# A macaron encoder block on one core: feed-forward openings in eight plain products with norms by token halves, x in row tiles, and the closing projection by token halves

## The reference, cut to what matters

```python
x = x + 0.5 * swiglu(rmsnorm(x, ffn1_norm), ffn1_w_gate, ffn1_w_up, ffn1_w_down)
h = rmsnorm(x, mix_norm)                      # one projection of h feeds both branches
merged = sigmoid(gate_a) * window_attention(...) + sigmoid(gate_b) * rwkv7(...)
x = x + merged @ w_out                        # "project-out"
x = x + cross_attention(rmsnorm(x, cross_norm), rmsnorm(mem, mem_norm))   # ends with @ w_co
x = x + 0.5 * swiglu(rmsnorm(x, ffn2_norm), ffn2_w_gate, ffn2_w_up, ffn2_w_down)
return rmsnorm(x, final_norm)
# rmsnorm(x, g) = x * rsqrt(mean(x * x) + 1e-6) * g
# swiglu(h, wg, wu, wd) = (silu(h @ wg) * (h @ wu)) @ wd
```

## Time and profile before

| | us |
|---|---|
| three runs: median (lowest to highest) | 3220.22 (3218.71 to 3220.97) |
| the profiled execution: its time | 3219.02 |
| the profiled execution: its span, first to last instruction | 3217.2 |

### The profile page before, as it was taken

How to read it: one execution, slowest core, us unless ns; L and a number is a source line. 1 busy time by engine, 2 the same in 40 slices (tenths; PEclk the granted TensorE clock), 3 DMA queues, 4 the chain that set the end, 5 groups by cost and what they waited for, 6 DMA issues and landing times. The chain is left out here.

```text
span 3217.2 us, 61692 instructions
## 1 busy us (share of the span) xinstructions
PE 2943.0 (91%) x26984; PEld 2412.2 (75%) x26984; DVE 1621.0 (50%) x1767; ACT 1087.4 (34%) x1780; POOL 1353.7 (42%) x705
## 2 busy tenths in 40 slices
PE   3799999996899999999999998899995799999995
PEld 2688888885677878778787887686774688887885
DVE  5654443445146666555666665243224645543445
ACT  2433333223234434334443333342212333333221
POOL 1344444443255555444555454462131344444441
PEclk7999999998999999999999999899997899999997
DMA  3222224442421211131121212351002222234441
GB/s 143 69 94 96 83 105 147 144 147 49 175 62 51 59 58 58 37 108 47 46 61 53 63 43 74 116 160 46 26 27 79 69 79 85 98 109 145 143 147 69
DMA packets 260169, 279.12 MB, mean 87 GB/s; under 512 B 13504, under 2 KB 213312, under 8 KB 257728
## 3 DMA queue, kind: packets, MB, share of 16 engines
q1 hardware_dynamic: 259904, 275.20, 26.2%
HBM read 224.83 MB, written 50.33 MB: 86 GB/s over the span
## 5 line engine op out<-in xcount | busy, mean ns | idle before, releaser
L483 POOL TENSOR_TENSOR w_low<-ffn_work,w_high 128x1024 fp32r<-128x1024 f32 x182 | 444.9, 2445 | 668.7 <-ACT w_high L556 395.4
L523 PE MATMUL bank<-h_high,w_high 128*128 128x512 f32 x1232 | 484.8, 393 | 59.1 <-DVE h_low L667 34.9
L523 PE MATMUL bank<-h_low,w_high 128*128 128x512 f32 x1232 | 483.4, 392 | 0.0
L523 PE MATMUL bank<-h_high,w_low 128*128 128x512 f32 x1232 | 483.4, 392 | 0.0
L1228 POOL TENSOR_TENSOR mix_panel_low<-arena,mix_panel_high 128x1024 fp32r<-128x1024 f32 x114 | 276.3, 2425 | 406.2 <-ACT mix_panel_high L1605 406.2
L1334 PE MATMUL bank<-mix_h_high,mix_panel_high 128*128 128x512 f32 (+1 forms) x896 | 357.7, 399 | 21.1 <-POOL mix_panel_low L1228 16.0
L1334 PE MATMUL bank<-mix_h_low,mix_panel_high 128*128 128x512 f32 (+1 forms) x896 | 342.0, 382 | 0.0
L1334 PE MATMUL bank<-mix_h_high,mix_panel_low 128*128 128x512 f32 (+1 forms) x896 | 340.7, 380 | 0.0
L714 DVE TENSOR_TENSOR h_low<-ffn_work,h_high 128x512 fp32r<-128x512 f32 x88 | 204.4, 2323 | 250.4 <-ACT h_high L571 250.4
L523 PEld LDWEIGHTS bank<-h_high,w_high 128*128 128x128 f32 x1232 | 234.1, 190 | 112.2 <-issue 61.4
L540 PE MATMUL bank<-h_high,w_high 128*128 128x512 f32 x704 | 274.8, 390 | 4.4 <-DVE h_low L714 4.4
(11 more groups left out here) (276 smaller groups left out, 5784.4 us busy)
## 6 DMA issues: line engine op xcount, KB each, us to landing
arena<-w_in SPq DMA_DIRECT2D x96, 512.0 KB, 3.8
ffn_work<-w_down SPq DMA_DIRECT2D x88, 512.0 KB, 3.6
a_spill<-ffn_work SPq DMA_DIRECT2D x88, 256.0 KB, 2.2
ffn_work<-a_spill SPq DMA_DIRECT2D x88, 256.0 KB, 2.6
ffn_work<-w_gate SPq DMA_DIRECT2D x12, 1024.0 KB, 5.7
ffn_work<-w_up SPq DMA_DIRECT2D x12, 1024.0 KB, 8.2
arena<-w_gate SPq DMA_DIRECT2D x10, 1024.0 KB, 5.6
arena<-w_up SPq DMA_DIRECT2D x10, 1024.0 KB, 8.2
```

Of the source, the lines that this page charges most:

```text
L483: nc.gpsimd.tensor_tensor(slot(w[1], q), src, slot(w[0], q).bitcast(F32), ALU.subtract).then_inc(s_low, 1)
L523: last = mm(bank[:, bk, :], w[wp][:, q % RING, kt, e], h[hp][:, k, kt], start=fresh and kt + wp + hp == 0, stop=kt == KT // 2 - 1 and wp = ...
```

## The change

It does four things.

- The first pair of each feed-forward is made of eight plain products (`FIRST`) of five weight panels; pairs 2 to 11 stay as they are. The five panels are rounded in the order A11, A12, A21, A22 and A11 again. The T sums are made later, beside these products, T2 in place.
- The norm at a feed-forward's opening is done by token halves. In the second feed-forward the first half's norm, the load of the first weights and the first panel's two parts lie in the cross stage; the block of the feed-forward begins with the second half's sums (`nrm[1]`).
- x comes in eight tiles of 128 rows, three places in turn; ACT squares a row tile with an accumulated sum, so the first feed-forward's norm needs no squares of xT and no sums on PE. The block ahead of it is gone: its work stands in the feed-forward's block (`front`). The first weights come in two halves of the columns, the constants other than the identity later. x goes to `x_spill` in parts (`keep_x`).
- The closing projection keeps panels 0 and 1 for both halves and then goes through panels 2 to 7 for the first half of the tokens and again for the second: 14 units instead of 8 panels. In project-out and here DVE, not POOL, makes the panels' low parts.

`lowered(q)` is q + 1, less one in the second feed-forward. Beside this, buffers that were opened in the mixer and cross stages are opened once for the whole kernel, and the constant `keep` is made from 64 columns by one copy.

The diff, cut to this core:

```diff
...
+FIRST_PANELS = [A11, A12, A21, A22, A11]
+C11, C21, C22, C12 = (0, 1), (4, 5), (6, 7), (2, 3)
+FIRST = [(0, B11, C11, True), (1, B21, C11, False), (2, B11, C21, True), (3, B21, C21, False),
+         (1, B22, C12, True), (3, B22, C22, True), (2, B12, C22, False), (4, B12, C12, False)]
+NQ0 = len(FIRST_PANELS)
...
+            def load_rows():
+                def tile(t):
+                    if t >= 3:
+                        sp.wait_ge(s_sq, t - 2)
+                    sp.dma_start(tiles[t % 3], d["x"][t * P:(t + 1) * P, :]).then_inc(s_tile[t % 3], 16)
+
+                def first_weights(fh):
+                    for e, src in enumerate((wg, wu)):
+                        sp.dma_start(raw[0][:, :, e, fh * P:(fh + 1) * P],
+                                     src[:, :, fh * P:(fh + 1) * P]).then_inc(s_first[fh], 16)
+
+                def keep_x(j):
+                    sp.wait_ge(s_placed, 4 * j + 4)
+                    cols = slice(2 * j * P, 2 * (j + 1) * P)
+                    sp.dma_start(x_view[:, :, cols], xT[:, :, cols]).then_inc(s_kept_x[j // 2], 16)
+
+                at, n = where["ident"]
+                sp.dma_start(cst[:, at:at + n], d["consts"][:, at:at + n]).then_inc(s_ident, 16)
+                for t in range(3):
+                    tile(t)
+                sp.dma_start(par[:], d["params"].rearrange("p (a b) -> p a b", a=NPAR)).then_inc(s_par, 16)
+                first_weights(0)
+                tile(3)
+                keep_x(0)
+                tile(4)
+                keep_x(1)
+                for t in range(5, 8):
+                    tile(t)
+                first_weights(1)
+                sp.dma_start(cst[:, n:], d["consts"][:, n:]).then_inc(s_rest, 16)
+                sp.dma_start(par_u[:], d["params_u"][:, :]).then_inc(s_rest, 16)
+                keep_x(2)
+                keep_x(3)
+
+            if front:
+                load_rows()
+            keep_act(0, 0)
+            keep_act(0, 2)
+            sp.wait_ge(s_blow, low_at["T2"])
+            sp.wait_ge(s_bsum, sums_before["T2"])
             load_group(1)
-            for g in range(GROUPS):
-                keep_act(g, 0, 0, 0, post[0])
-                keep_act(g, 1, 1, 1, post[4])
+            sp.wait_ge(s_low, lowered(NQ0 - 1))
+            load_group(2)
+            keep_act(0, 1)
...
+            if front:
+                nc.gpsimd.memset(minus_half_c[:], -0.5).then_inc(s_eps, 1)
+                pool.wait_ge(s_eps, 1)
+                nrm[0].pool_root(pool)
+                subtract_low(0, block_of(0, FIRST_PANELS[0]))
+            else:
+                nrm[1].pool_root(pool)
+            for q in range(1, NQ0):
+                subtract_low(q, block_of(0, FIRST_PANELS[q]))
+                if front and q == 1:
+                    nrm[1].pool_root(pool)
...
+            def turn_tile(t):
+                pe.wait_ge(s_tile[t % 3], 16 * (t // 3 + 1))
+                for j in range(2):
+                    if t < 4:
+                        b = (2 * t + j) % 6
+                        if t >= 3:
+                            pe.wait_ge(s_placed, 2 * (t - 3) + j + 1)
+                    else:
+                        b = 2 + j
+                        pe.wait_ge(s_placed, 2 * (t - 1) + j + 1)
+                    for i in range(4):
+                        kt = 4 * j + i
+                        last = nc.tensor.transpose(bank[:, b, i * P:(i + 1) * P],
+                                                   tiles[t % 3][:, kt * P:(kt + 1) * P], c("ident"))
+                    last.then_inc(s_turned, 1)
+
+            def first_product(r):
+                q, k, banks, fresh = FIRST[r]
+                closing = r in (1, 3, 6, 7)
+                for e in range(2):
+                    if e == 0 and q >= PRE:
+                        pe.wait_ge(s_low, lowered(q))
+                    if r == 4 and e == 0 and front:
+                        pe.wait_ge(s_placed, 16)
+                    elif r == 5:
+                        pe.wait_ge(nrm[1].done, KT * (nrm[1].n0 + 1))
+                    for kt in range(KT // 2):
+                        if e == 0 and front and r < 2:
+                            nrm[0].wait(pe, 4 * r + kt)
+                        elif e == 0 and r in (4, 6):
+                            pe.wait_ge(s_blow, low_at["B22" if r == 4 else "B12"] + kt + 1)
+                        for wp, hp in ((0, 0), (0, 1), (1, 0)):
+                            last = mm(bank[:, banks[e], :], slot(wp, q)[:, 2 * kt + e], operand(hp, k)[:, kt],
+                                      start=fresh and kt + wp + hp == 0,
+                                      stop=closing and kt == KT // 2 - 1 and wp == 1, skip_group_check=True)
+                    last.then_inc(s_prod, 1)
+                    if not front and r == 0 and e == 0:
+                        nrm[1].pe_scale(pe)
...
+            if front:
+                pe.wait_ge(s_ident, 16)
+                for t in range(4):
+                    turn_tile(t)
+                nrm[0].pe_scale(pe)
+            else:
+                nrm[1].pe_sums(pe)
+            for r in range(len(FIRST)):
+                first_product(r)
+                if front and r < 2:
+                    turn_tile(4 + 2 * r)
+                    turn_tile(5 + 2 * r)
+                elif front and r == 2:
+                    nrm[1].pe_scale(pe)
...
+            if front:
+                for t in range(4):
+                    square_tile(t)
+                round_first(0)
+                nrm[0].act_high(act, range(0, 2))
+                round_first(1)
+                nrm[0].act_high(act, range(2, 6))
+                place_tile(4)
+                nrm[0].act_high(act, range(6, 8))
+                place_tile(5)
+                square_tile(4)
+                square_tile(5)
+                round_first(2)
+                for t in (6, 7):
+                    place_tile(t)
+                for t in (6, 7):
+                    square_tile(t)
+            else:
+                round_first(1)
+                round_first(2)
+            round_input("B22")
+            round_first(3)
+            round_input("B12")
+            first_silu(0)
+            round_input("T1")
+            first_silu(2)
+            round_input("T3")
+            round_first(4)
+            round_input("T2")
+            round_weights(NQ0)
+            first_silu(1)
+            round_weights(NQ0 + 1)
+            first_silu(3)
+            round_weights(NQ0 + 2)
+            round_input("T4")
+            for g in range(1, GROUPS):
...
+            if front:
+                for t in range(4):
+                    for j in range(2):
+                        dve.wait_ge(s_turned, 2 * t + j + 1)
+                        V.tensor_copy(xT[:, 4 * j:4 * j + 4, t * P:(t + 1) * P],
+                                      bank[:, (2 * t + j) % 6, :].rearrange("p (a b) -> p a b", b=P)).then_inc(
+                                          s_placed, 1)
+                dve.wait_ge(s_sq, 4)
+                nrm[0].dve_spread(dve)
+                dve.wait_ge(s_par, 16)
+                dve.wait_ge(s_kept_x[0], 32)
+                nrm[0].dve_scale(dve)
+                dve.wait_ge(s_sq, 8)
+            nrm[1].dve_spread(dve)
+            dve.wait_ge(s_kept_x[1], 32 * (done + 1))
+            for j, name in enumerate(("B22", "B12")):
+                for kt in range(KT // 2):
+                    nrm[1].scale_tile(dve, 4 * (1 - j) + kt)
+                    if kt > 0:
+                        input_low(name, kt - 1)
+                input_low(name, KT // 2 - 1)
+            dve.wait_ge(nrm[1].done, KT * (nrm[1].n0 + 1))
+            input_sum("T1", half_of(0, 0), half_of(0, 1), half_of(0, 0))
+            input_sum("T3", half_of(0, 1), half_of(1, 1), half_of(0, 1))
+            first_multiply(0)
+            input_lows("T1")
+            first_multiply(2)
+            input_lows("T3")
+            input_sum("T2", half_of(1, 1), half_of(1, 1), half_of(0, 0))
+            input_lows("T2")
+            weight_sum(1, S1)
+            weight_sum(1, S3)
+            first_multiply(1)
+            input_sum("T4", half_of(1, 0), half_of(1, 0), half_of(1, 1))
+            weight_sum(1, S2)
+            first_multiply(3)
+            input_lows("T4")
...
+    UNITS = [(0, 0), (0, 1), (1, 0), (1, 1)] + [(o, n) for n in range(2) for o in range(2, KT)]
+    CLOSE = 2 + 2 * (KT - 2)
+    FFN_PANEL = CO + CLOSE
...
-            for k in range(CO, CO + KT):
+            for k in range(CO, CO + 4):
                 load(sp, k)
+            sp.wait_ge(s_o, 2 * XH)
+            for e, w in enumerate((panels(d["w_gate2"]), panels(d["w_up2"]))):
+                sp.dma_start(ffn_raw[:, :, e], w[:, :, 0:2 * P]).then_inc(s_ffn, 16)
+            for k in range(CO + 4, CO + KT + 2):
+                load(sp, k)
+
+            def keep_x(n, j, at):
+                sp.wait_ge(s_padd, Q + at)
+                rows = slice(4 * j, 4 * j + 4)
```

(56 more changed lines are left out.)

632 lines of the change are left out of this document (321 added, 311 removed).

## The result

| | before | after |
|---|---|---|
| median of four runs, us | 3220.59 (3218.71 to 3223.2) | 3142.79 (3140.06 to 3145.86) |
| profiled execution: time, span | 3219.02, 3217.2 | 3144.46, 3142.7 |
| first marker (third pair, first feed-forward) | 169.42 | 142.58 |
| first add of the closing projection | 2373.25 | 2346.69 |
| second marker | 2588.43 | 2513.61 |

What follows compares the result with a forecast made beforehand. PE was taken to bound the kernel wherever it has operands, with time to win where feed-forwards open. Gains of 24.9 and 50.1 us, 75.0 in sum, took 3219.02 to 3144.0, hence 3145 for the median; range 3130 to 3158 (68%).

Steps and rivals of the forecast that it cites:

- The first feed-forward: Start to first marker: the new opening moves the marker from 169.42 to 144.5, a gain of 24.9 us.
- the closing stage with the second feed-forward: First to second marker: second marker at 2538.3 instead of 2588.43, a gain of 50.1 us.
- DVE's chain: First feed-forward: DVE lowers inputs, takes sums T1, T3, T2 and frees x at 91.4; pair 1 starts at 103.7.
- the prediction's first rival: First feed-forward: its two order waits don't arise; idling of 11.8 + 8.6 + 2.7 and two cold starts go; 3118 us; 10%.
- The second rival: Both feed-forward openings: DVE sets them, its chain to the freed x taking 9 to 10 us more each; 3164 us; 17%.
- The lock: Both openings: meeting POOL's low half, the spread copy takes 2.62 us instead of 0.43; without it, 2.2 us earlier each.
- Project-out: Panel lows move from POOL to DVE; PE is busy there already, so 0, between -1 and +2 us.
- panel 10: Closing projection: its load lands near 2419.2 behind x, PE idles 2.6 us; landing before 2394 would be wrong.
- a cold start costs 1.7 us: PE's clock after an idle time near 8 us or more: 1.7 us lost, counted as 1.9.
- The third rival: Plain products and closing units: the clock stays at 1.2 GHz, +134 us less 6 counted; 3273 us; 3%.
- a clock under 0.9 in the eight products: Sign of being wrong: a clock under 0.9 in the eight plain products opening a feed-forward.
- The fourth: Both feed-forwards: nothing gained, as pair 1 waits for its weights as long as before; 3220 us; 2%.

Runs made afterwards that it cites:

- root later: Changed kernel with GpSimd taking the root of the second token half after panel 2's low half in the first feed-forward; median 3136.46 us.
- three moves: Changed kernel with the second half's root behind panel 2's low half, second weights ahead of tile 7, panel 10's load ahead of the x write; median 3126.01 us.
- panel 3 first: Changed kernel with ACT's rounding of panel 3 moved ahead of its rounding of input block B22, in both feed-forwards; median 3148.64 us.
- panel 3 first, weights early: Changed kernel with the second half's root behind panel 2's low half, panel 3 rounded ahead of B22, second weights issued ahead of tile 7; median 3138.97 us.

## Why the prediction was right, and where its terms were off

The forecast was 3145, the result 3142.8; at the second marker 75.0 us were predicted and 74.8 came. Behind that stand two errors of 2 us that cancel, so a part of the closeness is luck. (The medians differ by 77.8 us, the two profiled spans by 74.5; the terms are compared with the latter.) The first feed-forward won 26.8, not 24.9, and the closing stage with the second feed-forward 48.0 (the shift of the second marker less that of the first), not 50.1.

**The first feed-forward.** Its steps came as written: tile 3's transposes at 12.7, scaling at 20.9 (near 20), product 0 at 23.1 (near 22), product 1's end 41.2 (41.0), product 2 at 55.6 (55.0), product 3 at 71.6 (71.9). PE idled 11.4 and 8.3 us there, 11.8 and 8.6 predicted. The mis-sized term is DVE's chain behind it: x was free at 88.2, not 91.4. On that way DVE met POOL once in its trace (1.85 us for a half low instead of 0.69, at 70.22); the prediction allowed 28.1 us from 63.3 and doesn't write out how much of it was for locks, 24.8 were needed. From the load to pair 1 it took 13.2 us instead of 12.0 (8.5 + 1.1 + 2.4; the recorded 103.7 is 0.3 above its own terms), 1.1 of the difference being POOL's low half with 3.47 us. Pair 1 started at 101.45. The runs make a rule of the chain, from DVE's first scaling of the second half over the load to pair 1 and the marker:

| run | scaling | load issued | pair 1 | marker |
|---|---|---|---|---|
| changed kernel | 63.43 | +24.8 | +13.2 | +41.1 |
| root later | 55.56 | +24.8 | +13.2 | +41.1 |
| three moves | 48.72 | +24.8 | +13.2 | +41.1 |
| panel 3 first | 63.84 | +25.9 | +13.1 | +43.0 |
| panel 3 first, weights early | 51.23 | +25.9 | +13.0 | +44.0 |

(each time counted from the one before). PE's idle stretches appear in it only as the cold start behind them: 1.9 us after 11.4 us of idling (nine slow matmuls) and 2.9 after 11.2 (some fourteen), in the last two rows. That is the weak point of the prediction's first rival: it summed 11.8 + 8.6 + 2.7 and two cold starts to 26.9 us. With the chain, removing the first wait is worth what it moves DVE's scaling, and removing the second is worth nothing; the best run has 14.8, with a wait of 8.3 us still in place. The second rival, DVE as the bound, was right as a mechanism and wrong in size: DVE did set pair 1 of the first feed-forward, but 3 us earlier than I had it, not later.

**The lock.** The copies took 2.56 and 2.59 us beside POOL and 0.43 alone (2396.36), as the earlier trace rows has it. But "2.2 us earlier in each feed-forward" without it was wrong for the time of the kernel, by the run that took the lock away: nothing. In the first opening the write of x to memory ended later, a wait that the prediction did not put there; in the second the slow half product hid it. The Trainium skill ("SBUF — State Buffer", section Who interferes with whom) states that whichever of the two engines issues first keeps the shared port pair for its whole instruction; the trace agrees, with POOL's subtraction from 2427.57 to 2429.94 and the copy from 2427.64 to 2430.23. Once the clock was held up, its absence brought 1.3 us (3.1 less 1.8), and in the run with the second weights ahead of tile 7 PE waited 1.24 us for such a copy.

**Project-out.** Predicted 0 between -1 and +2: the stretch of fourteen products went from 80.69 to 80.52 us, and with the lows back on GpSimd 81.29. Right.

**The closing projection.** SP's order made panel 10 late as worked out: ACT got it at 2392.85, predicted 2392.6 (2419.2 less the 26.6 of shift). That is before the 2394 that the prediction named as a sign of being wrong; the sign was set with a shift of 25 and is tripped by the larger shift alone.

```profile
2392.85 1.06 ACT L2263 ACTIVATE panels_high<-cross_work 128x1024 fp32r<-128x1024 f32 x1 [9.07 <-DMA cross_work<-w_co]
```

PE waited 2.67 us (2.6). What failed is the clock: "a cold start costs 1.7 us, counted as 1.9 after an idle time near 8 us or more". The wait of 2.7 us cost 1.8 more, and that of 3.0 us at the end of the block 2.4 (twelve matmuls 0.2 us slow). The first of the two is not certain: of eight executions with that wait, seven have a granted clock of 0.90 over the two units and one, with panel 3 first, 1.00. Product 0 therefore began at 2426.2, not 2423.6 (2450.2 less 26.6). From there to pair 1 it took 46.4 us, and the prediction's 43.5, a wait of 1.5 and the scale of 1.0 make 46.0: the slow first half stands where the wait was expected. Against this the cold start of 1.0 counted for pair 1 did not come, as PE had no gap ahead of it: at 2472.61 the products had just ended, and the weights had been ready 1.3 us before.

```profile
2468.57 2.70 POOL L549 TENSOR_TENSOR w_low<-arena,w_high 128x1024 fp32r<-128x1024 f32 x1 [8.54 <-ACT w_high L689]
```

DVE, expected 0.7 late at the end of the units, did not hold the stage: without the wait for panel 10 it ended 4.4 us earlier.

**The third rival, the clock for whole stages,** did not arise: the granted clock is 0.94 in the eight products of the second feed-forward and 1.00 in products 4 to 7 of the first (79.20 to 101.40). But "a clock under 0.9 in the eight products" was a sign of being wrong, and over all eight of the first feed-forward (23.14 to 101.45) it is 0.79. It lies in products 0, 2 and 3, where the sum had counted cold starts, so the sign was set too sharply for its own sum. The fourth did not either. The unseen costs came out at their low ends: ACT places a transposed bank in 0.53 us (1.07 for two), DVE in 0.65 to 0.69, and the halved weights landed 7.0 us after their issue behind half a MB of x, as taken.

**What carries the 48.3 us of the second opening.** Norming the first token half under the units 10 (shown), starting on it while the other is normed 9 (shown), each undone by itself; that the two add up is not shown. If they do, the rest is 29 us and was not taken apart: it holds the pair 1 load that no longer waits behind the whole norm (11.5 us of PE's waiting before, and its cold start), the weights' load hidden under the closing units, and the squares done there; how it divides stays open. The 26.8 us of the first opening were not taken apart by a run either; the steps of the sum are confirmed there one by one, not what each part of the change is worth.

## What to carry to other kernels

Before you add up the idle stretches of the bounding engine, follow the chain that feeds the next fixed point, here from the norm over DVE to a freed buffer and a 2 MB load: a wait on that chain is worth its length, one beside it nothing (8.3 us removed, and the way to the marker became 2.9 us longer). Put short loads that the next unit needs ahead of long writes in a queue that works in order. Where something is found that costs nothing, ask what hides it, and try again when the cover is gone.

## What the runs showed of the hardware that I had not expected

- PE's clock can fall in shorter waits than I had counted. After 2.67 us of waiting, matmuls of 128x512 came 0.427 us apart (1.2 GHz) instead of 0.23 (2.4 GHz), granted clock 0.90 over the two units, 1.00 without the wait; after 3.02 us twelve of them. It need not: in one of eight executions a wait of 2.66 us at the same place left it at 1.00. Waits of 1.1 us (in the filled run) and 1.9 us (with the norm behind the units) left it up. Twelve matmuls that compute nothing, put into the 3.0 us, made the stretch 1.8 us shorter. The Trainium skill ("TensorE: Matmul & The Clock Gate", section Part 1: The HAM clock gate) has the clock follow how busy PE has lately been; the trace agrees, with these 0.427 and 0.23 us.
- The port shared by DVE and GpSimd moves time between their instructions in ways that an edit elsewhere shifts: POOL's low half of a 128x1024 panel took 2.3 to 4.5 us, and four of DVE's low halves 2.49, 3.92, 4.28 or 4.69, with the same shapes.
- A stretch of 2204 us in which no instruction was changed differed by 7 us between profiled executions of the variants, more than most edits here moved.
